# Halves of a projection tile around the next head's transposes, and two ones products in place of three

## The reference

```python
mod = silu(c) @ w_ada + b_ada                       # shift, scale, gate, twice
h = rmsnorm(x) * (1 + scale1) + shift1
proj = h @ w_in                                     # A: q|k|v, B: q|k|v, gate_A, gate_B
oa = diff_attention(rope(rmsnorm(qa)), rope(rmsnorm(ka)), va)     # 8 heads, two 64-d maps each
# B, 16 heads: stick-breaking, strictly causal
log_rest = where(mask, log_sigmoid(-z), 0)
after = lax.cumsum(log_rest, axis=3, reverse=True) - log_rest
w = where(mask, exp(log_sigmoid(z) + after), 0);  ob = w @ vb
mix = sigmoid(gate_A) * (oa @ w_oa) + sigmoid(gate_B) * (ob @ w_ob)
x = x + gate1 * (mix @ w_out)
x = x + gate2 * hier_moe(rmsnorm(x) * (1 + scale2) + shift2)      # top 2 of 32 experts
```

## Time and profile before

| | us |
|---|---|
| runs, median of 3 | 822.73 (819.91 to 823.5) |
| the profiled execution | 823.22 |
| its span, first to last instruction | 821.4 |
| PE busy | 702.3 (85% of the span) |
| DVE, ACT, POOL busy | 352.0, 270.8, 94.7 |

### The profile page before, as it was taken

One profiled execution on the slowest core, in us unless ns is written; L12 is line 12 of the kernel. 1 busy time (PEld: TensorE's weight loads), 2 busy tenths in 40 slices (PEclk: granted clock), 3 DMA queues, 4 the chain that ended last, 5 costly groups with the idle time before them and its releaser, 6 DMA issues.

```text
span 821.4 us, 13826 instructions
## 1 busy us (share of the span) xinstructions
PE 702.3 (85%) x5345; PEld 565.7 (69%) x5345; DVE 352.0 (43%) x552; ACT 270.8 (33%) x500; POOL 94.7 (12%) x158
## 2 busy tenths in 40 slices
PE   0798899998799999999988999878999897788770
PEld 0387788887689999999978999755565444454430
DVE  1555767777443433444323356542423232223225
ACT  0444555554443445554334542300111011011110
POOL 2012222222000000001100000011011001100011
PEclk9899999999999999999988999878999999999995
DMA  9957377764636795332315447789799999999916
GB/s 320 340 149 227 121 233 216 223 213 134 206 103 181 186 290 150 106 105 80 94 33 165 128 132 286 278 356 358 303 417 417 417 417 419 417 418 417 385 67 192
DMA packets 131176, 199.17 MB, mean 242 GB/s; under 512 B 11688, under 2 KB 113464, under 8 KB 117816
## 3 DMA queue, kind: packets, MB, share of 16 engines
q1 hardware_dynamic: 123032, 185.63, 63.9%
q0 software_dynamic: 6208, 11.02, 4.0%
q10 hardware_dynamic: 1888, 1.86, 0.8%
HBM read 193.47 MB, written 16.55 MB: 256 GB/s over the span
## 4 chain that ended last, share of the span: by engine, by line
PE 41%; DMA 16%; DVE 13%; ACT 10%; issue 8%; SPq 4%; DVEq 4%; ACTq 2%; POOL 1%; POOLq 0%
PE ps L575 18%; DMA e_w<-in_w 14%; PE ps L570 7%; PE ps L572 6%; PE ps L571 6%; ACT w_hi L1119 4%; SPq L507 3%; DVE w_lo L1432 2%; DMA vec_rows<-in_norm_g 2%; DVE w_lo L1440 1%; ACT probs L1217 1%; SPq L512 1%; DVE amap L1501 1%; ACT sig_r L1236 1%; ACT probs L1188 1%
## 5 line engine op out<-in xcount | busy, mean ns | idle before, releaser
L575 PE MATMUL ps<-e_w,xgT 128*64 128x256 f32 x1024 | 127.5, 408 | 27.8 <-issue 19.8
L575 PEld LDWEIGHTS ps<-e_w,xgT 128*64 128x64 f32 x1024 | 83.3, 147 | 67.7 <-issue 24.8
L570 PE MATMUL ps<-hT_hi,w_hi 128*128 128x320 f32 x320 | 102.4, 320 | 4.4 <-DVE w_lo L1432 4.2
L1432 DVE TENSOR_TENSOR w_lo<-raw,w_hi 128x2048 fp32r<-128x2048 f32 (+1 forms) x26 | 68.1, 2619 | 81.1 <-ACT w_hi L1119 81.1
L572 PE MATMUL ps<-hT_hi,w_lo 128*128 128x320 f32 x320 | 99.5, 311 | 0.0
L571 PE MATMUL ps<-hT_lo,w_hi 128*128 128x320 f32 x320 | 99.4, 311 | 0.0
L1764 DVE TENSOR_SCALAR h_s<-h_e 128x256 f32<-128x256 f32 x16 | 4.7, 294 | 156.0 <-ACT h_e L1349 156.0
L570 PEld LDWEIGHTS ps<-hT_hi,w_hi 128*128 128x128 f32 x320 | 60.7, 190 | 7.1 <-issue 4.0
L1119 ACT ACTIVATE w_hi<-raw 128x2048 fp32r<-128x2048 f32 (+1 forms) x26 | 56.4, 2168 | 21.7 <-PE ps L572 21.7
L571 PEld LDWEIGHTS ps<-hT_lo,w_hi 128*128 128x128 f32 x320 | 60.8, 190 | 0.0
L572 PEld LDWEIGHTS ps<-hT_hi,w_lo 128*128 128x128 f32 x320 | 60.7, 190 | 0.0
(11 more groups left out here) (260 smaller groups left out, 1267.6 us busy)
## 6 DMA issues: line engine op xcount, KB each, us to landing
e_w<-in_w SPq DMA_DIRECT2D x96, 1024.0 KB, 23.3
raw<-in_w_in SPq DMA_DIRECT2D x45, 512.0 KB
ada_late<-in_w_ada SPq DMA_DIRECT2D x16, 1024.0 KB, 6.4
ada_first<-in_w_ada SPq DMA_DIRECT2D x8, 1024.0 KB, 21.5
raw<-in_w_in SPq DMA_DIRECT2D x8, 1024.0 KB
raw<-in_w_oa SPq DMA_DIRECT2D x4, 1024.0 KB
raw<-in_w_ob SPq DMA_DIRECT2D x4, 1024.0 KB
raw<-in_w_out SPq DMA_DIRECT2D x4, 1024.0 KB
```

What stands on the lines that cost most here:

```text
L570: nc.tensor.matmul(out, lhs_hi, rhs_hi, start=first, stop=False, skip_group_check=True)
L575: return nc.tensor.matmul(out, lhs, rhs, start=first, stop=last, skip_group_check=True)
L1432: V.tensor_tensor(w_lo[j][:, :, 0:width], raw[j][:, :, 0:width], f32(w_hi[j][:, :, 0:width]), ALU.subtract).then_inc(split_done, 1)
```

## The change

Stage A:

- In steps 1 to 3 `proj_sample` waits for the load of `raw` instead of `split_done`. The wait for `split_done` moves to tile 0, which needs the split.
- In steps 3 to 7, where PE has both a projection and an output of head h-3, tile 1 is cut into halves of the depth: 12 products stand ahead of the q and k transposes and 12 behind them.
- In the steps with an output of head h-3 (3 to 8), ACT does `split_second` right after `split_first`, ahead of its copy of q and k; DVE does its first pass of the split ahead of its copy of q and k, the second pass behind it.

Stage B: the second key block's rows and the third key block's rows are multiplied by `ones_neg` in one product of 128 columns, and the third block's in one more of 64, in place of three of 64.

```diff
-                    pe.wait_ge(split_done, S_A + h + 1)
+                    if isinstance(h, int):
+                        pe.wait_ge(raw_loaded[j], 48 * ((h + 1) // 2))
+                    else:
+                        pe.wait_ge(split_done, S_A + h + 1)
                     pe.wait_ge(a_staged, 3 * h - 2)
...
-            def proj_tile(h, j, t, first):
-                if first and t == 0:
-                    pe.wait_ge(split_done, S_A + 1)
-                if not first:
+            def proj_tile(h, j, t, first, ks=range(KD)):
+                if t == 0:
+                    pe.wait_ge(split_done, S_A + h + 1)
+                if not first and 0 in ks:
                     pe.wait_ge(a_staged, 3 * h - 1 + t)
-                for k in range(KD):
+                for k in ks:
...
-                last.then_inc(a_proj, 1)
+                if KD - 1 in ks:
+                    last.then_inc(a_proj, 1)
...
                 early = isinstance(h, int) and h in (1, 2)
                 if P_on and early:
                     proj_tile(h, j, 1, False)
+                halves = P_on and o_on
+                if halves:
+                    proj_tile(h, j, 1, False, range(KD // 2))
                 if qk_on:
...
-                if P_on and not early:
+                if halves:
+                    proj_tile(h, j, 1, False, range(KD // 2, KD))
+                elif P_on and not early:
                     proj_tile(h, j, 1, isinstance(h, int) and h == 0)
...
                         mm(zs[:, 0:192], tri_neg, s, False)
-                        mm(zs[:, 0:64], ones_neg[:], s[:, 64:128], False)
-                        mm(zs[:, 0:64], ones_neg[:], s[:, 128:192], False)
-                        last = mm(zs[:, 64:128], ones_neg[:], s[:, 128:192], False)
+                        mm(zs[:, 0:128], ones_neg[:], s[:, 64:192], False)
+                        last = mm(zs[:, 0:64], ones_neg[:], s[:, 128:192], False)
...
                     split_first(jq, loaded, None if isinstance(h, int) and h == 0 else (a_proj, 3 * h), width)
+                    if o_on:
+                        split_second(jq, width)
                 if qk_on:
                     act.wait_ge(a_qkT, h)
                     A(qkT[:, 0:512], ps[:, 3, :], ACT.Copy).then_inc(a_qkT_act, 1)
-                if loaded is not None:
+                if loaded is not None and not o_on:
                     split_second(jq, width)
...
+                width = MIX_COLS if isinstance(h, int) and h >= 7 else UNIT
+                if split_on and o_on:
+                    split_part(h + 1, jq, h + 1, width, 0)
                 if qk_on:
                     dve.wait_ge(a_qkT, h)
                     V.tensor_copy(qkT[:, 512:1024], ps[:, 4, :]).then_inc(a_qkT_dve, 1)
                 if split_on:
-                    split_halves(h + 1, jq, h + 1, MIX_COLS if isinstance(h, int) and h >= 7 else UNIT)
+                    if not o_on:
+                        split_part(h + 1, jq, h + 1, width, 0)
+                    split_part(h + 1, jq, h + 1, width, 1)
```

More of the change, by code:

```diff
@@ L1433, in split, with split_part @@
                                 ALU.subtract).then_inc(split_done, 1)
-            def split_halves(s, j, nth, width):
[L1437 to L1442, removed]
+            def split_part(s, j, nth, width, n):
+                ks = slice(n * KD // 2, (n + 1) * KD // 2)
+                if n == 0:
+                    dve.wait_ge(split_half, nth)
+                else:
+                    dve.wait_ge(split_hi, s + 1)
+                last = V.tensor_tensor(w_lo[j][:, ks, 0:width], raw[j][:, ks, 0:width], f32(w_hi[j][:, ks, 0:width]),
+                                       ALU.subtract)
+                if n:
+                    last.then_inc(split_done, 1)
+            def split_halves(s, j, nth, width):
+                for n in range(2):
+                    split_part(s, j, nth, width, n)
             split(0, 0)
```

## The result

| | before | after |
|---|---|---|
| runs beside each other, median of 4 | 821.32 (818.38 to 823.5) | 806.81 (804.99 to 808.62) |
| ratio, 95% interval | | 0.983 [0.9803, 0.9857] |
| span of the profiled execution | 821.4 | 805.2 |
| granted clock of TensorE, mean | 0.948 | 0.954 |

The change gains 14.5 us by the medians and 16.2 between the two profiled spans. The forecast was 812.1, its range began at 808.4: the sign was right, the gain too small.

A forecast was written before the change was run, and what follows sets the result against it. PE, busy 85% of the span and leading the chain of waits, was taken as the bound. From 823.22 us, -1.33 + 0.7 - 2.1 - 5.4 - 3.0 = -11.1 gave 812.1 us, range 808.4 to 816.6.

The forecast's parts named there:

- Step 1, -1.33: Stage A, step 1: the sample projection starts 1.33 us earlier, no longer waiting for DVE's split; all of it stays.
- Step 3, -2.1: Stage A, step 3: 12 products instead of 24 behind the second transposes, 2.1 us less; lower bound 1.54.
- Step 8, nothing: Stage A, step 8: copies come later, but DVE opens the next maximum at the same time; no gain or loss.
- Step 2, +0.7: Stage A, step 2: 1.0 us gained, 1.68 charged for a clock fall behind PE's new stop; net 0.7 lost.
- The rival that the clock stays up: Stage A, step 2: no clock fall behind the stop, so 1.0 us gained; 810.4 us in all, chance 0.18.
- Steps 4 to 7, 4 x -1.34: Stage A's loop: both PE stops at the transposes go, L719 to L747 takes 5.50 us against 6.84; 1.34 less per step.
- Stage B, 16 x -0.19: Stage B, two heads in eight pairs: two ones products take 0.42 us in place of 0.61; 3.0 us less.
- Copies: Rival in stage A: PE waits for the copies of q and k, five steps lose 0.5 each; 814.7 us, chance 0.14.
- slower: Rival in steps 3 to 7: the series ending in DVE's copy of q runs 3.7 us longer; 828 us, chance 0.03.
- loads: Rival in steps 4 to 7: a step's transfers cannot shift with PE, half the gain stays; 814.8 us, chance 0.05.
- stops only move: Rival in stage A: PE's stops move behind the transposes, the 5.4 and 2.1 go; 819.6 us, chance 0.05.
- rule of columns: Rival in stage B: products' price goes by width, 128 + 64 costs three times 64, no gain; 815.1 us, chance 0.05.

The follow-up runs named there:

- the seven profiles with the early projection: Profiles of kernels whose sample projection no longer waits for the split, step 2's stop unfilled: three without a clock fall, two 1.6 us more, two 2.8 more.
- the stop filled: Kernel before, with unread products in PE's stops: 8 in step 2, 12 in step 9, 10 in stage B's last pair; 816.83 us, ratio 0.9945.
- The two measured ratios: The changed kernel against the kernel before, measured twice: 806.81 us, ratio 0.983, and once more unchanged, 807.77 us, ratio 0.9859.
- the filled pair: Kernels before and changed, both with unread products in the stops of step 2, step 9 and stage B's last pair: ratios 0.9945 and 0.9802.
- stage A alone: Kernel before with the whole change of stage A, stage B keeping three ones products: 814.13 us, ratio 0.99.

## Why the prediction was wrong

- **Step 1, -1.33**: right, 1.43, with the start-up at the low clock as in the profile that the sum was made from. **Step 3, -2.1**: right, 2.04, with the second transposes still waiting 0.70 for `oT_lo`. **Step 8, nothing**: right, for the reason given.
- **Step 2, +0.7**: this is the step that failed. "I take it that the clock falls there once more" was drawn from two stretches of one profile. In the changed kernel's profile the clock stayed at 1.00, and 1.01 was gained instead of 0.7 lost, 1.7 us. The rival that the clock stays up had this, at 0.18. Over the seven profiles with the early projection it came out as forecast in two (1.6 - 1.0 = 0.6 lost), worse in two (2.8 - 1.0 = 1.8 lost) and the other way in three, a mean of 0.2 lost. So one outcome was taken for certain in the sum where the runs show three. Nor did "most of that loss" fall into a wait in the kernel before: from the score products to the amap transposes it takes 85.96 - 67.21 = 18.75 us with the fall and 17.74 with the stop filled, so 1.0 of the 1.68 counted.
- **Steps 4 to 7, 4 x -1.34**: right mechanism, 1.455 each. From L719 to L747 I had 5.50, with 0.09 for starting each run of products anew; the trace has 5.39. Undersized by 0.45 in all.
- **Stage B, 16 x -0.19**: right mechanism, 0.22 each, since two calls together take 0.39 and not 0.42. Undersized by some 0.55 us.
- **What the sum left out**, the other step that failed: the clock in places that the change doesn't touch. The profiled execution of the kernel before, against which the sum was made, had it fall in step 2, step 9 and the last pair. In the changed kernel's profile the last pair's block ran at 1.00, 3.39 - 0.44 = 2.9 us; step 9 took 0.64 back. No term and no bound of the range stood for this. Why the clock stayed up there is open.
- **The base**: 823.22 lies 1.5 to 2.6 over the medians of the kernel before in the later comparisons (820.6 to 821.7). The steady 12.8 us from 821.3 give 808.5, just inside the range.
- **Copies, slower, loads, stops only move, rule of columns**: none came about. The copies were 0.47 us early; a step of 18.17 us with PE busy throughout leaves no room for slower, loads and stops that only move, and the block of 3.49 us none for the rule of columns. Two figures of the rivals are a little off and change nothing: the series of the copies ends 125.1 - 120.11 = 5.0 us on and not 5.1, and their case adds up to 814.6 and not 814.7.

The loop's and stage B's part is shown by the periods, which came back to the hundredth (18.17 and 18.00 us), step 3's by 19.29 and 19.33 us from step 2's amap transposes in the two profiles of the changed kernel; step 1's holds with the start-up at the low clock. The two measured ratios give 11.6 to 14 us, the filled pair 11.7. So of the 16.2 us between the two profiles about 12.8 belong to the edits, and most of the rest is what the clock did in those two executions. How the clock's part divides in the other executions behind the medians is not shown.

## What to carry to other kernels

Sum a change in steady periods, and keep the clock's falls apart: list the stops of PE behind which the granted clock is 0.5 in the profile, price each both ways, and put the sum of both ways into the range, also for stops that the change doesn't touch. When a stop is filled, the next one down the line should be known: here half of the loop's gain was held by the split until its passes were moved too. Float32 products of 64 columns are worth merging: here one cost 0.20 us and one of 128 columns 0.22, while 192 cost 0.33.

## What the runs showed that was not expected

A stop of PE of the same length, with the same work ahead of it, is followed by 2.4 GHz in one execution and 1.2 GHz in another: 2.98 us in step 2 (1.00 in the changed kernel, 0.53 with stage A alone). The same kernel can differ from itself, as the stretch from 192 to 197 us shows (1.00 and 0.66). The Trainium skill (TensorE: Matmul & The Clock Gate, "What's actually happening") says that the clock gate's watch runs freely and isn't reset when a kernel starts. No run here shows this; outcomes that differ between executions of one kernel don't speak against it.

A filler is no free insurance: at 2.4 GHz 12 products took 2.84 us and fit the stop of step 9, and where the clock was already low 10 took 4.47 and held back by 1.6 us what they were to protect.
